# Norm ends with the mean taken off early, ScalarE's squares and diagonals, and the search for keys dealt out by width

## The reference

```python
for i in range(2):
    h = layer_norm(ALPHA * h + 0.5 * swiglu(h, ffa_w_in[i], ffa_w_out[i]), ...)
    mix = hybrid_mixer(h, ...)     # gated delta rule, stick-breaking and latent attention
    h = layer_norm(ALPHA * h + mix, ...)
    h = layer_norm(ALPHA * h + 0.5 * swiglu(h, ffb_w_in[i], ffb_w_out[i]), ...)
    h = h + sigmoid(h @ ple_w_gate[i]) * (p[i] @ ple_w_proj[i])
x = h
x = x + 0.5 * m[2] * rmsnorm(swiglu_2(modulate(rmsnorm(x, g), m[0], m[1]), ...), g_post)
proj = modulate(rmsnorm(x, g), m[3], m[4]) @ w_in
# attention over the 256 best keys of each query, by an indexer's score; a gated recurrence beside it
x = x + m[5] * rmsnorm(merged @ w_out, g_post)
x = x + 0.5 * m[8] * rmsnorm(swiglu_2(modulate(rmsnorm(x, g), m[6], m[7]), ...), g_post)
```

## Time and profile before

| | |
|---|---|
| time, median of 3 runs | 3891.69 us (3886.96 to 3891.75) |
| the profiled execution | 3893.39 us, its span 3891.6 us, mean granted clock 0.959 |
| busy share of the span | PE 92%, PEld 71%, DVE 45%, ACT 31%, POOL 12% |
| granted PE clock in 40 slices, tenths | 9999999999999899999989899999999899889998 |
| DMA | 83 GB/s mean; a load of 512 KB lands 3.3 us after its issue |

### The profile page before, as it was taken

The page is one execution under the profiler, slowest core; times in us unless marked ns, Lnnn a source line. Parts: engine busy times, 40 slices in busy tenths (PEclk is TensorE's granted clock), DMA queues, the critical chain, the costliest instruction groups (busy, mean ns, idle before and its releaser), DMA issues. The chain is left out here.

```text
span 3891.6 us, 47323 instructions
## 1 busy us (share of the span) xinstructions
PE 3575.5 (92%) x19778; PEld 2767.7 (71%) x19778; DVE 1757.6 (45%) x2168; ACT 1217.8 (31%) x1752; POOL 479.8 (12%) x418
## 2 busy tenths in 40 slices
PE   7999899898999799999989899987999889779997
PEld 5888665776787578877658578865788666447886
DVE  5642355446542455323545555324333348643332
ACT  2232334233222322223342322224322253433221
POOL 0002001430003000020024300021000110330001
PEclk9999999999999899999989899999999899889998
DMA  4332111013332233321100133312233122112331
GB/s 155 135 126 91 60 63 36 3 45 114 134 120 72 80 137 137 112 77 65 64 14 3 60 130 139 111 51 79 92 98 105 52 73 69 33 49 92 92 104 59
DMA packets 88178, 324.22 MB, mean 83 GB/s; under 512 B 12696, under 2 KB 14744, under 8 KB 87584
## 3 DMA queue, kind: packets, MB, share of 16 engines
q1 hardware_dynamic: 87968, 321.21, 24.5%
HBM read 319.06 MB, written 2.12 MB: 83 GB/s over the span
## 5 line engine op out<-in xcount | busy, mean ns | idle before, releaser
L178 DVE TENSOR_TENSOR w_low<-w_raw,w_high 128x1024 fp32r<-128x1024 f32 (+2 forms) x496 | 638.1, 1287 | 1255.6 <-ACT w_high L171 1255.0
L171 ACT ACTIVATE w_high<-w_raw 128x1024 fp32r<-128x1024 f32 (+2 forms) x496 | 544.3, 1099 | 1432.3 <-PE ffa_ps L196 454.3
L194 PE MATMUL ffa_ps<-ffa_x_high,w_high 128*128 128x512 f32 x704 | 282.8, 402 | 35.1 <-DVE ffa_x_low L240 31.5
L194 PE MATMUL ffb_ps<-ffb_x_high,w_high 128*128 128x512 f32 x704 | 285.3, 405 | 24.1 <-DVE ffb_x_low L313 19.2
L194 PE MATMUL b_f_ps<-b_f_x_high,w_high 128*128 128x512 f32 x704 | 280.8, 399 | 18.4 <-DVE b_f_x_low L361 14.8
L195 PE MATMUL ffb_ps<-ffb_x_low,w_high 128*128 128x512 f32 x704 | 282.7, 402 | 0.0
L196 PE MATMUL ffb_ps<-ffb_x_high,w_low 128*128 128x512 f32 x704 | 281.5, 400 | 0.0
L195 PE MATMUL ffa_ps<-ffa_x_low,w_high 128*128 128x512 f32 x704 | 281.1, 399 | 0.0
L196 PE MATMUL ffa_ps<-ffa_x_high,w_low 128*128 128x512 f32 x704 | 280.7, 399 | 0.0
L195 PE MATMUL b_f_ps<-b_f_x_low,w_high 128*128 128x512 f32 x704 | 279.4, 397 | 0.0
L196 PE MATMUL b_f_ps<-b_f_x_high,w_low 128*128 128x512 f32 x704 | 279.2, 397 | 0.0
(11 more groups left out here) (518 smaller groups left out, 6762.3 us busy)
## 6 DMA issues: line engine op xcount, KB each, us to landing
w_raw<-in_ffa_in SPq DMA_DIRECT2D x88, 512.0 KB, 3.3
w_raw<-in_ffb_in SPq DMA_DIRECT2D x88, 512.0 KB, 3.3
w_raw<-in_ffn_in SPq DMA_DIRECT2D x88, 512.0 KB, 3.5
w_raw<-in_mix_in SPq DMA_DIRECT2D x80, 512.0 KB, 3.3
w_raw<-in_ffa_out SPq DMA_DIRECT2D x32, 704.0 KB, 4.1
w_raw<-in_ffb_out SPq DMA_DIRECT2D x32, 704.0 KB, 4.1
w_raw<-in_ffn_out SPq DMA_DIRECT2D x32, 704.0 KB, 4.1
ffa_ada_raw<-in_w_ada SPq DMA_DIRECT2D x36, 512.0 KB, 4.3
```

Source lines behind the costliest of these rows:

```text
L171: act.activation(self.high[:, n % HALVES, :cols], self.raw[:, n % SLOTS, :cols], ACT.Copy).then_inc(self.rounded, 1)
L178: dve.tensor_tensor(self.low[:, n % HALVES, :cols], self.raw[:, n % SLOTS, :cols], self.high[:, n % HALVES, :cols].bitcast(F32), ALU.subtr ...
L194: pe.matmul(out, w_high, x_high[:, k0 + k, :], start=start and place == 0, stop=False)
```

## The change

It has five parts. In the norms, the mean is copied to SBUF by ScalarE as soon as it is known and taken off the first four chunks in the norm's tail (two on VectorE, two on GpSimd), the other four at the next front; `shift` is gone. In ModulatedHalves the product with the factor goes from GpSimd to VectorE. In RmsResidual, ScalarE squares from PSUM and VectorE's copy applies the weight; GpSimd only adds, the last square goes to TensorE by itself, the two VectorE operations behind the factor are 1024 wide, SquareSum sums eight squares on TensorE without GpSimd, and the output leaves in four DMAs inside b2_f2. In the attentions ScalarE makes the diagonals, two activations for each unit. In the search, the steps are dealt out over blocks 10 to 24 by their width: a strike counts 2(t+1), a score or a mark t+1. The blocks then hold: 8 scores and 2 strikes of tile 1; 6 strikes; 6 strikes; 2 strikes, the mark and 5 scores of tile 2; 3 scores and 2 strikes; 4, 5 and 4 strikes; 1 strike, the mark and 4 scores of tile 3; 4 scores and 1 strike; four times 3 strikes; 3 strikes and the mark.

```diff
@@ NormHalves
     PARTS = ((0, 1), (1, 2), (2, 4), (4, 6), (6, 8))
+    CENTRED = 4
...
-        n_low = 0
+        n_low, n_centred = 0, 0
         for part, (begin, end) in enumerate(self.PARTS):
             h = self.h[:, begin:end, :]
+            if begin >= self.CENTRED:
+                dve.tensor_tensor(h, h, repeat(self.mean, 1, end - begin), ALU.subtract).then_inc(self.centred, 1)
+                n_centred += 1
+                low(n_low)
+                n_low += 1
+                dve.wait_ge(self.centred, n_centred)
             dve.tensor_tensor(h, h, repeat(self.rstd, 1, end - begin), ALU.mult).then_inc(self.scaled, 1)
             if part > 1:
                 low(n_low)
                 n_low += 1
-            dve.wait_ge(self.scaled, part + 1)
-            dve.tensor_tensor(h, h, repeat(self.shift, 1, end - begin), ALU.subtract).then_inc(self.shifted, 1)
-            if n_low < begin:
-                low(n_low)
-                n_low += 1
@@ ModulatedHalves
     def gpsimd(self, pool):
-        for k in range(KD):
-            at_least(pool, self.ready, k - 1)
-            pool.tensor_tensor(self.buffers[k % 2], self.x[:, k, :], self.r[:, :], ALU.mult).then_inc(self.scaled, 1)
+        pass
...
     def vector(self, dve, x_high, x_low):
-        for k in range(KD):
-            dve.wait_ge(self.rounded, k + 1)
-            dve.tensor_tensor(x_low[:, k, :], self.buffers[k % 2], x_high[:, k, :].bitcast(F32), ALU.subtract)\
-                .then_inc(self.ready, 1)
+        for k in range(KD + 1):
+            if k < KD:
+                at_least(dve, self.ready, k - 1)
+                dve.tensor_tensor(self.buffers[k % 2], self.x[:, k, :], self.r[:, :], ALU.mult).then_inc(self.scaled, 1)
+            if k:
+                dve.wait_ge(self.rounded, k)
+                dve.tensor_tensor(x_low[:, k - 1, :], self.buffers[(k - 1) % 2], x_high[:, k - 1, :].bitcast(F32), ALU.subtract)\
+                    .then_inc(self.ready, 1)
@@ LayerNorm
+        pool.wait_ge(self.mean_ready, 1)
+        for m in range(2, NormHalves.CENTRED):
+            pool.wait_ge(self.squared, m + 1)
+            self.centre(pool, m)
...
         act.activation(self.var[:, :], self.p_mean[:, :], ACT.Square, scale=1.0 / D).then_inc(self.mean_squared, 1)
+        act.activation(self.mean, self.p_mean[:, :], ACT.Copy, scale=1.0 / D).then_inc(self.mean_ready, 1)
...
+        dve.wait_ge(self.mean_ready, 1)
+        for m in range(2):
+            self.centre(dve, m)
         beside()
-        dve.wait_ge(self.inverted, 1)
-        dve.scalar_tensor_tensor(self.shift, self.p_mean[:, :], 1.0 / D, self.rstd, ALU.mult, ALU.mult).then_inc(self.shifted, 1)
@@ PairAttention
-            dve.wait_ge(self.inverted, n)
-            dve.tensor_tensor(self.diag[:, slot, :, :], repeat(self.ident, 1, 2), repeat(self.inverse[:, slot, :], 2, P), ALU.mult)\
-                .then_inc(self.diag_ready, 1)
...
+        if 0 < n <= self.count:
+            slot = (n - 1) % self.RING
+            act.wait_ge(self.inverted, n)
+            for a in range(2):
+                act.activation(self.diag[:, slot, a, :], self.ident, ACT.Copy, scale=self.inverse[:, slot, a:a + 1])\
+                    .then_inc(self.diag_ready, 1)
@@ SquareSum
     def tensor(self, pe):
-        total_squares(pe, self.sum, self.ones, self.pairs, self.summed, self.total_done)
+        for m in range(KD):
+            pe.wait_ge(self.squared, m + 1)
+            pe.matmul(self.sum[:, :], self.ones, self.square[:, m % self.RING, :], start=m == 0, stop=m == KD - 1)\
+                .then_inc(self.summed, 1)
@@ RmsResidual
+    PARTS = ((0, 2), (2, 4), (4, 6), (6, 8))
...
     def take(self, dve, m, ps):
-        return dve.tensor_copy(self.y[:, m, :], ps)
+        dve.wait_ge(self.squared, m + 1)
+        return dve.tensor_scalar(self.y[:, m, :], ps, self.weight[:, m:m + 1], None, ALU.mult)
...
+            first = self.square[:, 0, :] if m == 1 else self.total[:, :]
+            pool.tensor_tensor(self.total[:, :], first, self.square[:, m % 2, :], ALU.add).then_inc(self.summed, 1)
...
+        act.activation(self.square[:, m % 2, :], self.banks[m % len(self.banks)][:, :], ACT.Square).then_inc(self.squared, 1)
...
+        pe.wait_ge(self.summed, KD - 2)
+        pe.matmul(self.sum[:, :], self.ones, self.total[:, :], start=True, stop=False)
+        pe.wait_ge(self.squared, KD)
+        pe.matmul(self.sum[:, :], self.ones, self.square[:, (KD - 1) % 2, :], start=False, stop=True).then_inc(self.total_done, 1)
...
+        for part, (begin, end) in enumerate(self.PARTS):
+            y = self.y[:, begin:end, :]
+            dve.tensor_tensor(y, y, repeat(self.r[:, :], 1, end - begin), ALU.mult).then_inc(self.scaled, 1)
+            if part:
+                add(part - 1)
+        add(len(self.PARTS) - 1)
...
+    def sync(self, sp):
+        if self.out is not None:
+            for part, (begin, end) in enumerate(self.PARTS):
+                sp.wait_ge(self.added, part + 1)
+                sp.dma_start(self.out[:, begin:end, :], self.x[:, begin:end, :]).then_inc(self.out_stored, 16)
+            sp.wait_ge(self.out_stored, 16 * len(self.PARTS))
@@ KeySelection
+    def shares(self, count):
...
+        passes = {"score": 1, "strike": 2, "mark": 1}
+        done = list(itertools.accumulate(passes[kind] * (t + 1) for kind, t, _ in self.steps))
+        return [0] + [sum(d <= done[-1] * (k + 1) // count for d in done) for k in range(count)]
@@ build
-        second_block(nc, ws, h, mod, gains, const, t, norm)
-        load_small(nc, "finish", [(out, h[:, :, :])])
+        second_block(nc, ws, h, mod, gains, const, t, norm, out)
```

More of the change, by code:

```diff
@@ L14 @@
+import itertools
 import math
@@ L282 @@
 class NormHalves:
-    names = ["n_scaled", "n_shifted", "n_done", "x_rounded", "x_ready"]
+    names = ["n_centred", "n_scaled", "n_done", "x_rounded", "x_ready"]
     PARTS = ((0, 1), (1, 2), (2, 4), (4, 6), (6, 8))
+    CENTRED = 4
     def __init__(self, h, norm, gain, bias):
-        self.h, self.rstd, self.shift, self.gain, self.bias = h, norm[:, 0, :], norm[:, 1, :], gain, bias
+        self.h, self.rstd, self.mean, self.gain, self.bias = h, norm[:, 0, :], norm[:, 1, :], gain, bias
     def signals(self, *sems):
-        self.scaled, self.shifted, self.done, self.rounded, self.ready = sems
+        self.centred, self.scaled, self.done, self.rounded, self.ready = sems
     def gpsimd(self, pool):
@@ L398, in feed_forward @@
             finish.signals(taken, *sems[at:at + len(finish.names)])
+            finish.products(ws.used, lambda m: first + IN_BLOCKS + 2 * (m + 1), ps)
             if modulation:
@@ L650, in out_proj @@
             finish.signals(taken, *sems[at - 1:])
+            finish.products(ws.used, lambda m: first + m + 1, ps)
             @block.sync
@@ L708 @@
     names = ["firsts_added", "origin_done", "origin_ready", "moved", "centred", "squared", "sq_added", "sums_added", "mean_done",
-             "var_done", "mean_squared", "var_ready", "logged", "inverted", "shifted"]
+             "var_done", "mean_squared", "mean_ready", "var_ready", "logged", "inverted", "centred_end"]
     RING = 3
     def __init__(self, h, factor, norm, const, early, moved_first, last_added, origin_after, parts_after, squares_at):
-        self.h, self.factor, self.rstd, self.shift = h, factor, norm[:, 0, :], norm[:, 1, :]
+        self.h, self.factor, self.rstd, self.mean = h, factor, norm[:, 0, :], norm[:, 1, :]
         self.ones, self.eps = const["ones"], const["ln_eps"]
@@ L729, in allocate, with products @@
         self.p_origin, self.p_mean, self.p_var = bank("origin_ps"), bank("mean_ps"), bank("var_ps")
+    def products(self, used, done, banks):
+        pass
+    def sync(self, sp):
+        pass
     def take(self, dve, m, ps):
@@ L841, in inverse_root @@
     act.activation(r, r, ACT.Exp, scale=-0.5).then_inc(done, 1)
[L844 to L848, removed]
-def sum_squares(pool, pairs, square, squared, sq_summed, total_done):
-    for j in range(KD // 2):
-        pool.wait_ge(squared, 2 * j + 2)
-        at_least(pool, total_done, j - 1)
-        pool.tensor_tensor(pairs[:, j % 2, :], square[:, 2 * j % 3, :], square[:, (2 * j + 1) % 3, :], ALU.add)\
-            .then_inc(sq_summed, 1)
-def total_squares(pe, total, ones, pairs, sq_summed, total_done):
-    for j in range(KD // 2):
-        pe.wait_ge(sq_summed, j + 1)
-        pe.matmul(total[:, :], ones, pairs[:, j % 2, :], start=j == 0, stop=j == KD // 2 - 1).then_inc(total_done, 1)
 PLE_AHEAD = 6
@@ L2223, in first_mixer @@
     gdn_chunks(nc, name + "_gc", m, const)
-def load_small(nc, name, pairs):
-    with stage(nc, name, ["landed"]) as (block, landed):
-        @block.sync
-        def _(sp):
-            for dst, src in pairs:
-                sp.dma_start(dst, src).then_inc(landed, 16)
-            sp.wait_ge(landed, 16 * len(pairs))
 M2_X, M2_QI, M2_KI, M2_WI, M2_Q, M2_K, M2_V, M2_G = 0, 4, 8, 9, 10, 14, 18, 22
@@ L2259 @@
```

(20 more changed lines are left out.)

87 lines of the change are left out of this document (40 added, 47 removed).

## The result

The changed kernel takes 3852.32 us (median of 5 runs, 3850.51 to 3865.85) against 3891.69 (5 runs): a ratio of 0.9904, 95% interval 0.9888 to 0.9919. The forecast was 3852. Its profiled execution has a span of 3848.7 at a mean clock of 0.969, before 3891.6 at 0.959, so the two traces differ by 42.9, more than the medians (39.4). Single stages that nothing was changed in differ between the two traces by up to 3.5 (the second gated delta rule), and over all the traces of this document that stage ranges from 114.6 to 121.4. There is one trace for each kernel.

A forecast was written before the change was run, and what follows sets the result against it. TensorE, busy in 92% of the span, was taken as the bound, idling at stage joins and in the search. Terms summed to -39.8: profiled 3893.4 becomes 3853.6, and with the median 1.7 lower, 3852 us; range 3837 to 3874.

The forecast's parts named there:

- four joins into mix_proj and ffb: LayerNorm ends into mix_proj and ffb: longer tail, shorter front, -1.2 us each, -4.8 together; each between -3.7 and +1.
- two joins into ple: LayerNorm ends into ple: +1.3 and -2.2, so -1.0 us each, -2.0 together; each between -3 and +1.
- fronts of b2_f1, b2_proj, b2_f2: Stage starts: with the product on VectorE a chunk takes 1.5 us instead of 1.93; -0.2, -2.0 and -2.0.
- search, to the end of b2_proj: Search for keys, blocks 10 to 25: steps dealt by width leave about 1 us of stalls; -8.3 (-6 to -9).
- end of b2_f2 and output: -3.5 us at b2_f2's end, -3.0 as the last 512 KB piece lands in 3.3, -1.2 for the barrier; -7.8 with rounding.
- Tail (+2.1) and front (-2.2): At each mix_proj or ffb join, centrings lengthen the norm's tail by 2.1 us; the front up to the third x_low shortens by 2.2.
- from there on TensorE sets the pace: At the joins, past the third x_low, TensorE sets the pace; an earlier high clock was taken as 1.1 us per join.
- TensorE's waits for x_low: Sign to look for: at the two ffb joins these waits go from 19.2 us together to about 15.
- The ends of the residuals: Ends of b2_f1 and b2_mo: earlier VectorE start, wider operations, ones-products following in steps; -7.8 and -8.1 us.
- the 9.2 in 6 waits: In the search, TensorE's waits for w_low before the change, in us, 2.8 the longest; forecast to fall to about 1.
- The attentions: Diagonals on ScalarE: b2_att -2.6 us (-5 to +1); the two mix_ma +1.9 each, +3.8 together (0 to +9.6).
- rival A: Clock stays low through the ones-products: f1 and mo gain 4.3 less each, factor 5 more; -26, 3866 us, chance 0.14.

The follow-up runs named there:

- early scores: Changed kernel with TensorE's and ScalarE's part of the first three scores of tiles 2 and 3 one weight block ahead: 3848.71 us, ratio 0.9881.

## Why the prediction was right, point by point

The total was met to 0.3 us, and that is better than its parts, and than the spread of the five runs (15 us). The profiled execution came out at 3850.5, where the sum gave 3853.6. Each part is measured between two events of the two traces, us:

| step | forecast | measured |
|---|---|---|
| four joins into mix_proj and ffb, to the third weight block | -4.8 | -10.6 |
| two joins into ple, to the fifth weight block | -2.0 | +1.0 |
| factor stage | +2.0 | +1.9 |
| end of b2_f1 | -7.8 | -8.2 |
| end of b2_mo | -8.1 | -9.0 |
| fronts of b2_f1, b2_proj, b2_f2 | -0.2, -2.0, -2.0 | +0.6, -1.0, -1.0 |
| search, to the end of b2_proj | -8.3 | -6.7 |
| b2_att, whole stage | -2.6 | -4.0 |
| mix_ma, two | +3.8 | +5.7 |
| end of b2_f2 and output | -7.8 | -7.6 |
| sum | -39.8 | -38.9 |

The remaining 4.0 of the 42.9 lie in stretches that weren't changed, some shorter and some longer (the second ffa by 2.9).

- **The joins.** Tail (+2.1) and front (-2.2) were right to 0.1. To the end of the first two weight blocks the joins gained 1.0, 1.6, 1.7 and 1.7, near the 1.2 each. The step that failed is "from there on TensorE sets the pace": the four joins were forecast at -4.8 and measured -10.6, as I followed the join only to the first two blocks. Behind them TensorE pauses again, and the clock that used to fall there is worth another 1.55 in three of the four joins. The pause and the low stretch stood in the trace of before; a longer timeline would have shown them.
- **The joins into ple** show the same with the other sign. Up to the third weight block they gained 0.1 and 0.5. By the fifth the first of them has lost 1.55: the changed kernel's clock falls behind two pauses there (1310.8 to 1314.2 and 1321.1 to 1324.5), that of the kernel before behind one (1315.1 to 1318.5).
- **TensorE's waits for x_low** in ffb did not fall from 19.2 to about 15; they read 18.8 in 2 waits. The longer tail ahead of the barrier is counted into the same wait, so that row couldn't show what the front gained.
- **The ends of the residuals** were the best founded terms: a chain of single operations, each with its row.
- **The fronts.** Of the shorter chunk period I let 2.0 arrive at TensorE; 1.0 did in this trace. In b2_proj the fifth weight block ends 42.8 after the barrier before and 41.7 in the changed kernel, but 40.0 in four of the kernels above whose b2_proj begins alike (diagonals on VectorE, norm ends undone, four centrings on VectorE, early scores), with the clock low for 10 us in place of 14. So this term is no surer than 1.7. For b2_f1 the sign was wrong by 0.8: its w_low and first product follow one another on VectorE.
- **The search.** The step that failed is the 9.2 in 6 waits. The window began at 3196, and the first of these waits (2.07, for the product at 3197.19) lies ahead of block 10's end at 3203.07, before any strike, and is there in both kernels. Within the stretch it was 7.2, and it went to 2.7, not to about 1. Blocks 10 to 25, which the forecast was about, gave 5.8, and the last steps behind them 0.9. Also, the scores' order cost 2.9, which the sum by width doesn't see.
- **The attentions.** The bounds were right and both middles off, to opposite sides. At the head of b2_att TensorE's wait fell by 3.7, where I had 2.8. In mix_ma I had left the clock out: about half of the loss goes with it, as worked out under the diagonals.
- **The output.** A piece of 512 KB landed in 2.7, not 3.3.
- **A slip in rival A.** It adds 5 to the factor stage's +2.0, beyond the +5 given there as the bound; by that bound A is 3864.

That the errors cancelled (-5.8 at the four joins, -1.4 in b2_att and -1.3 behind b2_f1 and b2_mo against +3.0 in ple, +2.8 at the fronts, +1.9 in mix_ma and +1.6 in the search) is luck, though one with a bound. Each of the four joins stayed within its -3.7 to +1. Of the other terms only the first ple join left its range (+1.45, where +1 was the bound), and the search if blocks 10 to 25 alone are counted, by 0.2.

## What to carry to other kernels

Follow a join until the engine's steady state, not to its first instruction: over the four joins the pause behind the first two blocks was worth 4.6, the chain ahead of them 6.0. Where TensorE idles for a few us at every stage's start, products that nobody reads can be cheaper than a shorter chain (two of them, with the norms' ends as before, gave the changed kernel's ratio); try them before rebuilding the chain. Before work is shared out between VectorE and GpSimd, add up both as if they ran one after the other, and deal out dependent steps by who waits for whom, not by their sum alone. And before a stage's length is put down to an edit, compare the granted clock in it: the same code of mix_ma took 71.7 and 77.7 in one execution.

## What the runs showed of the hardware

Two VectorE subtractions with both inputs in SBUF took 3.18 beside two of GpSimd's, and all four took 2.35 on VectorE alone. TensorE's granted clock fell to its lower level right behind the pause after the first two blocks in three of four joins before the change and in none after it, where TensorE had come to the high level earlier; at the second mix_proj it held already before, so I can't give a rule from these rows. In the first ple it fell behind such pauses after the change too. Filling that pause with two products took the ratio from 0.9943 to 0.9904 and 7 us off the trace's span.
